# A four-layer network on one core: norms turned tile by tile, earlier routing, another order of tables, a sixth place for weights

## What is computed

```python
for i in range(2):                                   # first block
    u = h @ w_in[i]
    y_mla, y_diff, y_sb = mla_mixer(...), diff_mixer(...), sb_mixer(...)   # three kinds of attention
    mix = concatenate([y_mla, y_diff, y_sb]) @ w_o[i]
    h   = layer_norm(ALPHA * h + mix, ln1_g[i], ln1_b[i])
    ffn = grouped_moe(h, router_w, router_b, w_gate[i], w_up[i], w_down[i])  # 16 experts, 2 a row
    ple = sigmoid(h @ ple_gate[i]) * (p[i] @ ple_proj[i])
    h   = layer_norm(ALPHA * h + ffn + ple, ln2_g[i], ln2_b[i])
for l in range(2):                                   # second block
    a = gla_branch(...) @ w_branch[0]; b = gmlp_branch(...) @ w_branch[1]; c = moba_branch(...) @ w_branch[2]
    ga, gb, gc = split(sigmoid(gate part of h @ w_in_2[l]))
    h = layer_norm(ALPHA * h + (ga * a + gb * b + gc * c) @ w_out[l], ...)
    h = layer_norm(ALPHA * h + square(relu(h @ w_ff1[l])) @ w_ff2[l], ...)
```

## Time and profile before

| | before |
|---|---|
| median of 3 runs | 2003.84 us |
| the profiled execution | 2008.08 us |
| its span, first to last instruction | 2006.8 us |
| TensorE busy | 1825.2 us, 91% |
| VectorE busy | 1363.4 us, 68% |
| ScalarE busy | 1138.1 us, 57% |
| mean granted clock of TensorE | 0.962 |
| bytes moved | 413.17 MB, 206 GB/s |

### The profile page before, as it was taken

How to read it: one execution, slowest core, us unless ns; L and a number is a source line. 1 busy time by engine, 2 the same in 40 slices (tenths; PEclk the granted TensorE clock), 3 DMA queues, 4 the chain that set the end, 5 groups by cost and what they waited for, 6 DMA issues and landing times.

```text
span 2006.8 us, 27459 instructions
## 1 busy us (share of the span) xinstructions
PE 1825.2 (91%) x11220; PEld 1572.5 (78%) x11220; DVE 1363.4 (68%) x1591; ACT 1138.1 (57%) x1576; POOL 173.9 (9%) x152
## 2 busy tenths in 40 slices
PE   5978898999799889998878999989999999999998
PEld 4866777777587777776768889979898889988997
DVE  5576799899647579889875566565555556556555
ACT  4464588887636458878863644434444645434443
POOL 0000132311000003312110000000000000000000
PEclk9889899999889889999989999999999999999999
DMA  8314398999742348999884444645554544454552
GB/s 239 111 64 163 120 365 327 333 357 331 252 146 85 131 147 316 333 342 346 323 288 144 146 154 149 206 139 200 189 184 154 168 139 156 160 197 168 183 195 84
DMA packets 203011, 413.17 MB, mean 206 GB/s; under 512 B 16352, under 2 KB 118496, under 8 KB 186496
## 3 DMA queue, kind: packets, MB, share of 16 engines
q1 hardware_dynamic: 201792, 409.76, 59.2%
q10 hardware_dynamic: 1088, 1.57, 0.4%
HBM read 409.47 MB, written 1.84 MB: 205 GB/s over the span
## 4 chain that ended last, share of the span: by engine, by line
PE 67%; DVE 20%; ACT 6%; issue 2%; DMA 1%; POOL 0%; DVEq 0%; ACTq 0%
DVE weights_lo L389 12%; PE PS L404 9%; PE PS L408 9%; PE PS L405 9%; PE PS L412 7%; PE PS L415 6%; PE PS L416 6%; PE PS L1393 3%; PE PS L1396 3%; PE PS L1439 3%; PE PS L1418 3%; ACT weights_hi L384 2%; DMA arena<-in_w_down 1%; PE PS L1379 1%; DVE expert_rows_lo L1649 1%
## 5 line engine op out<-in xcount | busy, mean ns | idle before, releaser
L389 DVE TENSOR_TENSOR weights_lo<-weights_raw,weights_hi 128x1024 fp32r<-128x1024 f32 (+1 forms) x600 | 702.6, 1217 | 240.4 <-ACT weights_hi L384 238.0
L384 ACT ACTIVATE weights_hi<-weights_raw 128x1024 fp32r<-128x1024 f32 (+1 forms) x600 | 594.6, 1045 | 136.5 <-PE PS L416 84.4
L404 PE MATMUL PS<-hT_hi,weights_hi 128*128 128x256 f32 (+1 forms) x1488 | 428.6, 288 | 20.3 <-ACT weights_hi L384 11.4
L408 PE MATMUL PS<-hT_hi,weights_lo 128*128 128x256 f32 (+1 forms) x1488 | 425.8, 286 | 5.1 <-DVE weights_lo L389 5.1
L405 PE MATMUL PS<-hT_lo,weights_hi 128*128 128x256 f32 (+1 forms) x1488 | 425.4, 286 | 0.0
L404 PEld LDWEIGHTS PS<-hT_hi,weights_hi 128*128 128x128 f32 (+1 forms) x1488 | 285.9, 192 | 27.8 <-issue 14.5
L408 PEld LDWEIGHTS PS<-hT_hi,weights_lo 128*128 128x128 f32 (+1 forms) x1488 | 285.6, 192 | 6.9 <-DVE weights_lo L389 6.2
L405 PEld LDWEIGHTS PS<-hT_lo,weights_hi 128*128 128x128 f32 (+1 forms) x1488 | 286.0, 192 | 2.1
L412 PE MATMUL PS<-weights_hi,opa_hi 128*128 128x512 f32 x384 | 154.1, 401 | 8.3 <-DVE opa_lo L575 8.1
L415 PE MATMUL PS<-weights_lo,opa_hi 128*128 128x512 f32 x384 | 152.9, 398 | 0.0
L416 PE MATMUL PS<-weights_hi,opa_lo 128*128 128x512 f32 x384 | 152.8, 398 | 0.0
(11 more groups left out here) (322 smaller groups left out, 3203.3 us busy)
## 6 DMA issues: line engine op xcount, KB each, us to landing
weights_raw<-in_w_in SPq DMA_DIRECT2D x80, 1024.0 KB, 5.3
weights_raw<-in_w_ff SPq DMA_DIRECT2D x64, 1024.0 KB, 5.2
weights_raw<-in_w_up SPq DMA_DIRECT2D x42, 1024.0 KB, 7.1
weights_raw<-in_w_down SPq DMA_DIRECT2D x38, 1024.0 KB, 7.6
weights_raw<-in_w_gate SPq DMA_DIRECT2D x36, 1024.0 KB, 7.3
arena<-in_w_gate SPq DMA_DIRECT2D x14, 1024.0 KB, 7.0
params<-in_w_gate SPq DMA_DIRECT2D x14, 1024.0 KB, 7.0
arena<-in_w_down SPq DMA_DIRECT2D x14, 1024.0 KB, 7.7
```

The lines of the kernel that those rows point to most:

```text
L384: act.activation(u.flat[0][:, c:e], u.x[:, c:e], ACT.Copy).then_inc(*sig.mark("w_hi", u.u, i))
L389: dve.tensor_tensor(u.flat[1][:, c:e], u.x[:, c:e], u.flat[0][:, c:e].bitcast(F32), ALU.subtract).then_inc(*sig.mark("w_lo", u.u, i))
L404: pe.matmul(o, w[0], x[0], start=start, stop=False)
L408: return pe.matmul(o, w[1], x[0], start=False, stop=stop)
```

## The change

Six things change; the diff below holds their core.

1. **Norms.** `h` is written in halves of 512 columns with a signal each, and `turn_tile` waits for the half that it turns. VectorE makes `hT_lo` of tile 0 between *mean* and *gained* of tile 1, ScalarE makes `hT_hi` of tile 0 ahead of the squares of tile 1. A following product waits for the quarter that it reads.
2. **The first unit behind a norm.** Behind `ln2 1` and `ln2b 0` it is now `gla v0`, with rows on partitions (`project_tiles`), and its 24 products of tile 0 stand between the turnings of the two tiles. Behind `ln1` it is `ple gate 0`, whose four units have 256 columns by 1024 rows now in place of 512 by 512. Behind `ln2 0` and `ln1b` the first unit stays what it was, and behind the last norm nothing is turned.
3. **Routing.** VectorE routes right after the split of `ple gate 0`; gates, remainders of `h` and counts follow; `ple gate 3` stands between the counts and the slots on TensorE.
4. **Tables of layer 0.** The sines of block 0 go from behind the 4th bias copy on ScalarE to behind the 10th, those of block 1 ahead of the exponentials; the angle steps on VectorE go to the 8th and 13th bias step and have two tiles; the sign goes into the sine. The small inputs, 1 MB of `x` among them, are fetched behind the unit `mla 0`.
5. **A sixth place.** Expert units from the 9th on may also lie in another part of `arena`, the last ones of a layer too.
6. **Second block.** Another order of the units in the first half, and `split_merged(0)`, the remainder of the first half of the merged branches, ahead of the last half of the sums. The output goes out in four transfers of 256 KB in place of two of 512 KB.

```diff
-        for half in range(2):
-            halves(f"ple gate {half}", a["ple_gate"][l], 512 * half)
+        for i in range(4):
+            cols(f"ple gate {i}", a["ple_gate"][l], 256 * i)
...
         w = a["w_in_2"][l]
+        pair("gla v", w, GV)
         pair("gla q", w, GQ)
         pair("gla k", w, GK)
-        halves("gla v", w, GV)
         pair("gla g", w, GG)
...
                 late = of_expert(name) and not all(of_expert(n) for n, *_ in plan[u:u + 10])
-                n = NRAW if not of_expert(name) else NRAW + 1 if late else NRAW + 2
-                place = min(range(n), key=lambda i: -1 if last[i] is None else last[i])
+                allowed = list(range(NRAW)) + [NRAW] * (nth > 0) + [NRAW + 1] * (nth > 0 and not late) + [NRAW + 2] * (nth > 8)
+                place = min(allowed, key=lambda i: -1 if last[i] is None else last[i])
...
-                          (mem(11264, UNIT) if self.raw == NRAW else pslot)[:, 0:size])
+                          (mem(11264, UNIT), pslot, mem(4096, UNIT))[self.raw - NRAW][:, 0:size])
...
-                sp.wait_ge(*(sig.at("ps", f"mla y {l}") if u.raw == NRAW else sig.at("norm_dve", f"ln1 {l} new1")))
+                sp.wait_ge(*(sig.at("ps", f"mla y {l}"), sig.at("norm_dve", f"ln1 {l} new1"),
+                             sig.at("moe_dve", f"h and ple {l}"))[u.raw - NRAW])
...
+        def turn_tile(pe, label, t):
+
+            for half in range(2):
+                pe.wait_ge(*sig.at("norm_dve", f"{label} new{t}{half}"))
+                b = banks.hold(pe, f"{label} T{t}{half}", (4 + 2 * t + half,), "dve_took")
+                for j in range(4):
+                    k = half * 4 + j
+                    last = transpose(pe, PS[:, b, j * P:(j + 1) * P], h[:, t, k * P:(k + 1) * P])
+                last.then_inc(*sig.mark("ps", f"{label} T{t}{half}"))
...
+        def turned_lo(dve, label, t):
+            for half in range(2):
+                name, sl = f"{label} T{t}{half}", turned_slices(t, half)
+                dve.wait_ge(*sig.at("hT_hi", name))
+                lo_part(dve, hT[1][sl], one_bank(banks.of(name), 4), hT[0][sl]).then_inc(*sig.mark("dve_took", name))
...
                 if t == 0:
                     dve.wait_ge(*sig.at("params_in", label))
+                elif turned:
+                    turned_lo(dve, label, 0)
                 dve.wait_ge(*sig.at("norm_dve", f"{label} mean{t}"))
                 dve.scalar_tensor_tensor(gained[:, t, :], h[:, t, :], stat[t][:, 1:2], pslot[:, 0:D], ALU.add,
                                          ALU.mult).then_inc(*sig.mark("norm_dve", f"{label} gained{t}"))
...
-                dve.scalar_tensor_tensor(h[:, t, :], gained[:, t, :], stat[t][:, 4:5], pslot[:, D:2 * D], ALU.mult,
-                                         ALU.add).then_inc(*sig.mark("norm_dve", f"{label} new{t}"))
-
...
+                for c in (0, 512):
+                    dve.scalar_tensor_tensor(h[:, t, c:c + 512], gained[:, t, c:c + 512], stat[t][:, 4:5],
+                                             pslot[:, D + c:D + c + 512], ALU.mult, ALU.add).then_inc(
+                        *sig.mark("norm_dve", f"{label} new{t}{c // 512}"))
+                sig.also("norm_dve", f"{label} new{t}")
...
+                if i == 9:
+                    sines(0)
                 yield
-                if i == 3:
-                    sines(0)
-                    yield
...
-                if i == 6:
-                    angles(0)
+                if i in (8, 13):
+                    angles(i // 13)
...
+            def first_gate(t):
+                for k in range(KD):
+                    if k % 4 == 0:
+                        pe.wait_ge(*sig.at("dve_took", n_("ln1") + f" T{t}{k // 4}"))
+                    last = rows_still(pe, PS[:, gate0, t * S:(t + 1) * S], u, at_k(hT, k, t * P, (t + 1) * P),
+                                      at_k(u.pair, k, 0, S), k == 0, k == KD - 1, t == k == 0)
+                return last
+
+            first_gate(0)
+            turn_tile(pe, n_("ln1"), 1)
             pe.wait_ge(*sig.at("dve_took", n_("ln1") + " T11"))
...
+            first_gate(1).then_inc(*sig.mark("ps", n_("ple gate 0")))
+            pe.wait_ge(*sig.at("act_took", n_("router")))
+            b = banks.take(pe, n_("router T"), "dve_took", among=4)
+            for t in range(NT):
+                last = transpose(pe, PS[:, b, 16 * t:16 * t + 16], scT[0:16, t * P:(t + 1) * P])
+            last.then_inc(*sig.mark("ps", n_("router T")))
+            project_tiles(pe, (n_("ple gate 1"), n_("ple gate 2")), hT, "act_took", among=4)
...
+            feed(n_("ple gate 0"))
+            take_steps(route, 48)
+            feed(n_("ple gate 1"))
+            gate_rows(0)
             for t in range(NT):
                 dve.wait_ge(*sig.at("moe_act", n_(f"h hi {t}")))
-                lo_part(dve, h_split[1][:, t, :, :], h_strided[:, t, :, :], h_split[0][:, t, :, :]).then_inc(*sig.mark("moe_dve", n_("h split")))
-            for half in range(2):
-                for i in range(2):
-                    feed(n_(f"ple gate {half}{i}"))
-                if half == 1:
-                    take_steps(route, 48)
-                for t in range(NT):
-                    dve.wait_ge(*sig.at("act_took", n_(f"ple gate {half}") + f" t{t}"))
-                    v = ple[:, t, 512 * half:512 * half + 512]
-                    dve.tensor_tensor(v, v, sg_of(t), ALU.mult).then_inc(*sig.mark("ple_dve", n_(f"gated {half}{t}")))
+                lo_part(dve, h_split[1][:, t, :, :], h_strided[:, t, :, :], h_split[0][:, t, :, :]).then_inc(
+                    *sig.mark("moe_dve", n_("h split")))
+            feed(n_("ple gate 2"))
+            gate_rows(1)
             counts_vector(dve, l)
+            feed(n_("ple gate 3"))
+            gate_rows(2)
+            gate_rows(3)
...
                     feed(n_(f"branch {i}{half}"))
+                    if (i, half) == (2, 1):
+                        split_merged(0)
                     dve.wait_ge(*sig.at("act_took", n_(f"branch gate {i}{half}1")))
...
             if name == "mla 0":
                 if l == 0:
-                    small_sync(sp)
+                    lambda_sync(sp)
                 up_params(sp, l)
+            if name == "mla 1" and l == 0:
+                small_sync(sp)
...
             for t in range(NT):
-                sp.wait_ge(*sig.at("norm_dve", f"ln2b {DEPTH - 1} new{t}"))
-                sp.dma_start(out[0, t * P:(t + 1) * P, :], h[:, t, :]).then_inc(*sig.landing("out_stored", "all"))
+                for c in (0, 512):
+                    sp.wait_ge(*sig.at("norm_dve", f"ln2b {DEPTH - 1} new{t}{c // 512}"))
+                    sp.dma_start(out[0, t * P:(t + 1) * P, c:c + 512], h[:, t, c:c + 512]).then_inc(
+                        *sig.landing("out_stored", "all"))
```

## The result

| | before | after |
|---|---|---|
| median of 4 runs each | 2003.53 us | 1945.43 us (1943.74 to 1949.22) |
| ratio, with its 95% interval | | 0.9713 (0.9693 to 0.9733) |
| profiled execution | 2008.08 us | 1943.74 us |
| span | 2006.8 us | 1942.5 us |
| TensorE idle in the span | 181.6 us | 141.2 us |

The kernel became 58.1 us faster by the medians; 1949 was predicted. Sums over the profiles are therefore compared with 64.3, not with 58.1.

A forecast was written before the change was run, and what follows sets the result against it. It took TensorE, 91% busy, as the bound, with VectorE close in some stretches. Terms −19.2 − 13 − 8 − 5.9 − 9.2 = −55.3 us, from the median 2003.84, gave 1948.5, predicted as 1949; range 1936 to 1962, chance 0.55.

The forecast's parts named there:

- A: Tables of layer 0: three TensorE waits go, 11.2 + 5.2 + 2.8, −19.2 us; bounds −8 and −25.
- B: From `ln1` to the first expert: earlier routing removes a wait, −6.5 us in each of 2 layers, −13.
- C: Experts' end: the sixth place lets late units be asked for earlier, −4 us in each layer, −8.
- D: Norms and the end of the kernel: changed order around the turnings, −5.9 us in sum, mostly behind `ln2b 0`.
- E: Second block: waits for `opa_lo` and `weights_lo` go, 2.6 + 2.0 = 4.6 us a layer, −9.2 in the sum.
- So the 11.2 us go: Layer 0 tables: TensorE's 11.2 us wait for a projection's copy goes, unit fetched earlier and sines later on ScalarE.
- In the changed order the angles stand at the 13th bias step: Layer 0 tables: second angle block moves under projections, so TensorE's 5.2 us wait for MLA's rows goes.
- Rival 1: Layer 0 tables: bias comes back from HBM no earlier, so A is only −8 and the time 1960; chance 0.14.
- The remainder of `h` (2 of 1.2, 2.4 us): Behind the routing: 2.4 us of the about 14 us that VectorE must do before the slots' copy is done.
- since the last transfer leaves when half a *new* is done: End of the kernel: the last output transfer leaves earlier, worth −0.7 us.
- Rival 2: Holes refilled, clock falls anyway: B −2 a layer, C and D 0, A and E as forecast; 1972, chance 0.20.
- rival 3: Experts: six loads in flight lengthen every unit's split; slower than before from 12%, 2043 at 20%; chance 0.04.

The follow-up runs named there:

- t1: Changed kernel with the first sines back behind the 4th bias copy, their angle steps ahead of the 6th bias step; ratio 0.9744 to the kernel before.
- t3: Changed kernel with the small inputs, `x` among them, fetched ahead of the unit `mla 0` again, sines still late; ratio 0.9720 to the kernel before.
- t2: Changed kernel with the second block of angle steps back at the tables' end on VectorE, ahead of the bias mask; ratio 0.9698 to the kernel before.
- t8: Changed kernel with the split of `sb q`, second angle block, bias mask and lambdas all ahead of MLA's rows on VectorE; ratio 0.9730 to the kernel before.
- t4: Changed kernel without the sixth place for weights: five, and four for a layer's last units; ratio 0.9751 to the kernel before.
- s1: Kernel before with only the first merged half's remainder moved ahead of the last half of the sums, in both second-block layers; ratio 0.9958 to the kernel before.

## Why the prediction was right

The time, 1945.4, is 3.6 us from the 1949 predicted. A, B and C came out within 2 us of their terms; D and E together won 6.6 us more than theirs. Over the profiles the sum was 64.3 us against 55.3 predicted, 9 us more; that the medians lie only 3.6 us from the forecast is in part luck, since the profile of before, on which the working rests, was 4.6 us slow. Point by point:

- **A** was right in size, and the runs showed two of its reasons. "So the 11.2 us go": yes, as 7.4 for angles and sines (t1) and 3.0 for the unit (t3). The step "In the changed order the angles stand at the 13th bias step" was not the cause as the change stands: without it nothing is lost (t2). What makes it needless is that MLA's rows and the splits have changed places with the tail, which the prediction did not name (t8); whether the steps' place alone would have done it stays open. The next late thing was named rightly, the bias's return, with 7.4 us of VectorE's waiting, and it costs TensorE nothing. Rival 1 is therefore out in its result, though its mechanism is there.
- **B** was right in size (−6.9 and −6.7 for −6.5). "The remainder of `h` (2 of 1.2, 2.4 us)" was mis-sized: it takes 4.3 us, since it reads `h` in strides, and the profile of before had the same instructions at 4.5. The counts and the slots' copy take 0.8 in place of 1.5, so that VectorE needs 14.2 us from the end of the routing to the end of the slots' copy, as forecast; TensorE has 11.6 us of work there, and the new wait is 2.6 us where 3 to 4 were expected. The mixture was different, though: in the table's stretches only 3.2 and 3.0 us are idle time, where the forecast had 5.6, and 3.7 and 3.8 are busy time (less clock loss, and 2 us of idle matmuls), where it had 0.9. The row of the remainder, and that of the slots' copy:

```profile
198.24 4.29 DVE L605 TENSOR_TENSOR opa_lo<-h,opa_hi 128x1024 fp32r<-128x1024 f32 x2
209.20 0.40 DVE L1687 CAST slot_T<-PS 16x256 fp32r<-16x256 f32 x1
```

- **C** was right: −5.3 and −4.3 for −4 each. t4 loses 8.1 of these 9.6 us, and ScalarE's wait of 2.2 for the down unit comes back. Of the −4, 3 were to be idle time and 1 clock; measured were 2.1 and 3.2 in layer 0, 3.4 and 0.9 in layer 1.
- **D and E** were too small by 6.6 us in the sum (−21.7 measured from `ln2 0` to the end without B and C, −15.1 predicted). The two waits of the second block for `opa_lo` went, as s1 shows, and `ln2 0` lost 1.7 for +1: VectorE waits 2.3 us there within the norm, for turned copies that wait for TensorE's turning, which the prediction had named as a sign of being wrong. The stretch of `ln1b` 0, put at nothing, won 1.2. The output won 0.5 us for 0.7, from the last product to the end of the span (8.04 to 7.55), but the step "since the last transfer leaves when half a *new* is done" was wrong. The last transfer still leaves behind the whole *new*, whose halves take 0.75 us each; what is shorter is its landing. The Trainium skill's rule for transfers ("DMA: Bandwidth & Descriptors", "Bandwidth"), by which the end would have been worth nothing, did not decide: the four smaller output transfers take 2.1 us each against 2.7, which is the gain, less what the halves of *new* cost.

```profile
out_h<-h SPq DMA_DIRECT2D x4, 256.0 KB, 2.1
```

- **What was mis-sized is the clock.** In the sum 49 us were idle time and 6 were clock. Measured were 46.9 us of time without useful work (40.4 of idle time and 6.5 of idle matmuls), and 17.4 us of other busy time, nearly all clock by the estimate above. The granted clock's mean rose from 0.962 to 0.978. The forecast took something for it only behind the routing, the experts' end and `ln2b 0`. But the lower level also went from 30.7 us to 13.7 in A, and from 13.7 to none in the stretch of the second block-2 layer.

Rival 2 (holes refilled, 1972) is ruled out by the stretches and rival 3 (slower splits) by t4. Of the other signs, the down unit's wait, the clock behind `ln2b 0` (1.00), the bias mask and the remainders (1219 ns) spoke for the forecast; TensorE's two waits for `opa_lo` of 1.4 us, over the 1 us named, are those of the first block.

## What to carry to other kernels

Follow a wait back through the queue of the engine that ends it, and price what stands ahead there: that gave the sizes here, even where the reason within a term was wrong. Undo the parts one by one, and remember that this tells what a part is worth beside the others: for two edits at the same place (t2, t8), each has to be tried without the other. Where TensorE idles often, count for each hole also the products behind it at the lower clock; here that was more than a quarter of the gain. Before calling a fall in busy time clock, take off the instructions that are no longer executed. And look up the rows for every instruction that is moved: the two strided remainders had a row of their own, 1.8 times that of the plain ones.

## What the runs showed of the hardware

The same hole is not always paid for twice. In the profile of before, the wait for `opa_lo` comes once in each layer of the second block, 2.6 us and 2.6 us long; behind the first the granted clock stayed at 1.00, behind the second it was 0.50 for 3.4 us (columns as in the earlier trace rows):

```profile
1316.00:1319.40 3.40, 3.10 (x13) 2.54 (x14) 3.40 (x4) 2.10 (x3) 0.00 (x0) 1.00 0.06 18
1785.90:1789.30 3.40, 3.40 (x10) 2.66 (x9) 2.31 (x3) 0.68 (x1) 0.00 (x0) 0.50 0.01 2
```

Why it fell in one layer and not in the other, no run shows. This is a part of the 14.5 us that the second layer's stretch won, where the first won 7.1, and perhaps of why executions of one kernel differ by several us (1943.74 to 1949.22 for the changed one, on mean clocks of 0.978 and 0.972).

A change of function table costs ScalarE its load and nothing else where no other engine is waited for. In the changed kernel's first layer the load takes 1.28 us, starts within 0.02 us of the end of the activation before it, and the next activation starts 0.01 us behind its end:

```profile
84.35 1.28 ACT L782 ACT_TABLE_LOAD   x1
85.64 0.30 ACT L782 ACTIVATE lam<-lam 128x2 f32<-128x2 f32 x2
```

The Trainium skill ("ScalarE: Activation LUTs", "What ACT_TABLE_LOAD costs") would have put another 1.38 us behind each of the two table loads that went. This trace shows no such time. No run here takes a table load away by itself.
